# Attention's exponentials and values split into rounded parts and remainders, and a root moved ahead of a run of projection work

## What is computed

```python
def block(q):                                    # 128 queries
    s = einsum('bqkgd,bnkd->bkgqn', q, keys) * scale
    p = softmax(s)                               # over 1280 keys
    return einsum('bkgqn,bnkd->bqkgd', p, vals)
```

```python
o = rmsnorm(o_f + flip(o_b), gain)
return o * silu(g)
```

## Time and profile before

| | before |
|---|---|
| median of 3 runs | 3191.41 us |
| profiled execution | 3190.96 us, of which the span of the trace is 3189.1 us |
| granted TensorE clock, mean | 0.987 of full speed |
| DVE busy (VectorE) | 1543.6 us (48%) |
| ACT busy (ScalarE) | 1000.1 us (31%) |
| POOL busy (GpSimd) | 450.3 us (14%) |

### The profile page before, as it was taken

How to read it: one execution, slowest core, us unless ns; L and a number is a source line. 1 busy time by engine, 2 the same in 40 slices (tenths; PEclk the granted TensorE clock), 3 DMA queues, 4 the chain that set the end, 5 groups by cost and what they waited for, 6 DMA issues and landing times.

```text
span 3189.1 us, 36113 instructions
## 1 busy us (share of the span) xinstructions
PE 3046.8 (96%) x14927; PEld 2487.1 (78%) x14927; DVE 1543.6 (48%) x1907; ACT 1000.1 (31%) x1441; POOL 450.3 (14%) x352
## 2 busy tenths in 40 slices
PE   8899999989999999999989999999898999999997
PEld 6688888878788888888866668888776888888886
DVE  7566666553565553433566764456644122222224
ACT  5555555552311122212423332233322111111111
POOL 4333333321000001000300002133300000000001
PEclk9999999999999999999999999999999999999999
DMA  3111111122233431111210001101131111111111
GB/s 124 40 47 47 47 47 47 47 67 99 65 115 121 129 120 52 49 51 47 94 54 7 9 10 48 34 21 40 47 112 31 56 47 47 52 47 47 50 43 60
DMA packets 77235, 184.75 MB, mean 58 GB/s; under 512 B 7056, under 2 KB 29072, under 8 KB 77072
## 3 DMA queue, kind: packets, MB, share of 16 engines
q1 hardware_dynamic: 77072, 182.44, 18.2%
HBM read 163.87 MB, written 15.79 MB: 56 GB/s over the span
## 4 chain that ended last, share of the span: by engine, by line
PE 86%; DVE 8%; ACT 4%; issue 2%; POOL 0%; DMA 0%; POOLq 0%; DVEq 0%; SPq 0%; ACTq 0%
PE ps L512 39%; PE ps L1604 18%; PE ps L2950 8%; PE ps L2291 4%; DVE b L2899 2%; PE ps L2429 1%; PE ps L909 1%; PE ps L2255 1%; PE ps L2284 1%; PE ps L2283 1%; DVE b L501 1%; PE ps L916 1%; ACT b L493 1%; PE ps L86 1%; PE ps L891 1%
## 5 line engine op out<-in xcount | busy, mean ns | idle before, releaser
L512 PE MATMUL ps<-b 128*128 128x512 f32 x6024 | 1494.9, 399 | 35.6 <-DVE b L501 14.0
L512 PEld LDWEIGHTS ps<-b 128*128 128x128 f32 x6024 | 1109.9, 190 | 251.2 <-issue 19.9
L1604 PE MATMUL ps<-b 128*128 128x512 f32 x2592 | 599.1, 392 | 0.7 <-DVE b L1745 0.7
L1604 PEld LDWEIGHTS ps<-b 128*128 128x128 f32 x2592 | 485.0, 187 | 109.3 <-DVE b L1745 1.1
L501 DVE TENSOR_TENSOR b<-b 128x1024 fp32r<-128x1024 f32 (+1 forms) x206 | 255.3, 1241 | 288.3 <-ACT b L493 280.9
L493 ACT ACTIVATE b<-b 128x1024 fp32r<-128x1024 f32 (+1 forms) x206 | 214.9, 1045 | 515.9 <-PE ps L1604 427.4
L2950 PE MATMUL ps<-b 128*128 128x512 f32 (+1 forms) x1464 | 327.3, 379 | 6.8 <-ACT b L3010 5.9
L2950 PEld LDWEIGHTS ps<-b 128*128 128x128 f32 x1464 | 255.0, 192 | 56.5 <-issue 11.5
L1402 POOL TENSOR_TENSOR b<-b 128x1024 f32<-128x1024 f32 x18 | 43.2, 2399 | 916.8 <-ACT b L1433 916.4
L2291 PE MATMUL ps<-b 128*128 128x512 f32 x320 | 163.0, 592 | 0.0
L1761 DVE TENSOR_TENSOR b<-b,ps 128x1024 f32<-128x1024 f32 x64 | 78.1, 1220 | 152.4 <-PE ps L1604 152.3
(11 more groups left out here) (306 smaller groups left out, 3292.8 us busy)
## 6 DMA issues: line engine op xcount, KB each, us to landing
b<-in_down SPq DMA_DIRECT2D x52, 512.0 KB, 3.7
b<-in_mod SPq DMA_DIRECT2D x96, 256.0 KB, 2.7
b<-in_gu SPq DMA_DIRECT2D x44, 512.0 KB, 3.6
b<-scratch SPq DMA_DIRECT2D x38, 512.0 KB, 4.4
b<-in_dn_in SPq DMA_DIRECT2D x32, 512.0 KB, 5.1
b<-in_up SPq DMA_DIRECT2D x32, 512.0 KB, 3.8
b<-in_win SPq DMA_DIRECT2D x26, 512.0 KB, 3.7
scratch<-b SPq DMA_DIRECT2D x18, 512.0 KB, 2.9
```

The costliest lines, as they stand in the source:

```text
L512: ins = e.matmul(ps[:, c], w, h[:, k, c], start=first and k == 0 and i == 0, stop=last and k == KT - 1 and i == 2)
L1604: ins = e.matmul(ps[:, c], w, u[:, at[k], c], start=k == 0 and p == 0, stop=k == n - 1 and p == 2)
```

## The change

In the attention stage:

- The exponentials are taken twice: into an fp32 tile prob ("e") and into a rounded tile phi ("ex"). A subtraction makes the remainder plo = prob - phi ("lo"). VectorE does it for block 4 of every turn, behind the second half of the reciprocal; GpSimd does it for the other nine.
- The values are rounded when they are copied into vx, and VectorE makes their remainder vlo from PSUM in three subtractions at the start of `dve_attend`, behind a wait for all partition copies. GpSimd sets the middle of vlo to zero.
- The value matmul in fp32 becomes three in fp32r: vx with phi, vlo with phi, vx with plo; the third waits for "lo".
- Maxima 1 of the first turn wait for vlo instead of the copies.
- There are three phi and three plo tiles. The four prob tiles lie in two of the raw weight tiles, and SyncE loads the unit behind them after the stage. The reciprocal is written into the output tile ao, of which there is one, and the product is made in place.

In the gated attention, the six steps of projection work on ScalarE stand behind the root instead of ahead of its table.

```diff
+                self.phi, self.plo = ([sb([128, 512], F32R, at) for _ in range(3)] for _ in range(2))
+                self.vlo = sb([128, 10, 192], F32R, at)
+                self.ao = sb([128, 512], ctx=at)
+                free = [self.raw[(UNIT["win", 14] + i) % RAW] for i in range(2)]
+                self.prob = [r[:, 512 * i:512 * i + 512] for r in free for i in range(2)]
...
@@ pool_qkv
         self.after_qkv(e)
+        e.memset(self.vlo.bitcast(F32)[:, :, 64:128], 0.0).then_inc(*self.at[3].up("vz"))
@@ pe_attend
-                    e.wait_ge(*self.aq[1].at("tv", ("win", 5), 2))
+                    e.wait_ge(*V.at("vlo"))
...
-                e.matmul(O[i % 2], self.vx[:, b, 64 * g:64 * g + 128], self.prob[(t - 2) % 4], start=b == 0,
-                         stop=b == 9).then_inc(*P.up("pv", t - 2))
+                v, w = (x[:, b, 64 * g:64 * g + 128] for x in (self.vx, self.vlo))
+                e.matmul(O[i % 2], v, self.phi[(t - 2) % 3], start=b == 0, stop=False)
+                e.matmul(O[i % 2], w, self.phi[(t - 2) % 3], start=False, stop=False)
+                e.wait_ge(*(V if b in self.LOW else G).at("lo", t - 2))
+                e.matmul(O[i % 2], v, self.plo[(t - 2) % 3], start=False, stop=b == 9).then_inc(*P.up("pv", t - 2))
@@ act_attend
             if t >= 4:
-                e.wait_ge(*P.at("pv", t - 4))
-            e.activation(self.prob[t % 4], S[t % 3], ACT.Exp, scale=0.125).then_inc(*A.up("ex", t))
+                e.wait_ge(*(V if (t - 4) % 10 in self.LOW else G).at("lo", t - 4))
+            e.activation(self.prob[t % 4], S[t % 3], ACT.Exp, scale=0.125).then_inc(*A.up("e", t))
+            if t >= 3:
+                e.wait_ge(*P.at("pv", t - 3))
+            e.activation(self.phi[t % 3], S[t % 3], ACT.Exp, scale=0.125).then_inc(*A.up("ex", t))
+
+    LOW = (4,)
+
+    def attend_low(self, e, sig, t):
+        e.wait_ge(*self.at[1].at("ex", t))
+        if t >= 3:
+            e.wait_ge(*self.at[0].at("pv", t - 3))
+        e.tensor_tensor(self.plo[t % 3], self.prob[t % 4], self.phi[t % 3].bitcast(F32), ALU.subtract).then_inc(*sig.up("lo", t))
@@ dve_attend
+        for s in self.stack:
+            e.wait_ge(*s.end())
+        for j in range(3):
+            n = min(4, 10 - 4 * j)
+            e.wait_ge(*self.aq[1].at("tv", ("win", 5), j))
...
+            ins = e.tensor_tensor(parts(self.vlo), ps, parts(self.vx.bitcast(F32)), ALU.subtract)
+        ins.then_inc(*V.up("vlo"))
...
                 e.reciprocal(rec[r, 256:512], o[sums, 256:512]).then_inc(*V.up("rec", i - 1))
-                e.wait_ge(*V.last())
-                if i >= 5:
-                    e.wait_ge(*self.attst[(i - 1) % 4].at(i - 5, 1))
-                e.tensor_tensor(self.ao[((i - 1) // 2) % 2][r, :], o[r, :], rec[r, :], ALU.mult).then_inc(*V.up("of", i - 1))
+            if i < 16:
+                self.attend_low(e, V, 10 * i + 4)
+            if i:
+                e.wait_ge(*V.at("rec", i - 1))
+                e.tensor_tensor(self.ao[r, :], o[r, :], rec[r, :], ALU.mult).then_inc(*V.up("of", i - 1))
@@ pool_attend
             e.tensor_copy(self.qx[g][r], self.qs[g][r, :, qc].bitcast(F32)).then_inc(*G.up("qx", i))
+            e.wait_ge(*G.last())
+            for b in range(10):
+                if b not in self.LOW and i:
+                    self.attend_low(e, G, 10 * i - 10 + b)
+        for b in range(10):
+            if b not in self.LOW:
+                self.attend_low(e, G, 150 + b)
@@ act_gla
             e.activation(B["sq"], B["qf"], ACT.Square).then_inc(*A.up("osq", h))
-            side.fill(self.gla_fill(h, 6))
             self.act_roots(e, A)
             e.wait_ge(*V.at("oms", h))
             e.activation(small[:, 8:16], small[:, 0:8], ACT.Sqrt).then_inc(*A.up("ort", h))
+            side.fill(self.gla_fill(h, 6))
             side.until((h, "g"))
@@ SpSide
-        self.k.sp_weights(self.e, UNIT[u] + 5)
+        upto = UNIT[u] + 5
+        self.k.sp_weights(self.e, min(upto, UNIT["win", 14] + 3) if u[1] < 6 else upto)
```

More of the change, by code:

```diff
@@ L416, in memory @@
                 self.kx = [sb([128, TA], F32R, at, "right") for _ in range(2)]
-                self.vx = sb([128, 10, 192], ctx=at, side="right")
+                with ExitStack() as tmp:
+                    vz = sb([128, T], ctx=tmp, side="right")
+                self.vx = sb([128, 10, 192], F32R, at, "right")
                 self.amax, self.aneg = (sb([128, n], ctx=at, side="right") for n in (8, 72))
@@ L420, in memory @@
                     self.a_sq = [sb([128, T], ctx=tmp) for _ in range(2)]
-                    vz = self.vx.rearrange("p a b -> p (a b)")[:, 0:T]
                     z = [sb([128, TA], ctx=tmp), vz, sb([128, T], ctx=tmp)]
@@ L426, in memory @@
                 self.qx = [sb([128, 4, 128], F32R, at) for _ in range(2)]
-                self.prob = [sb([128, 512], ctx=at) for _ in range(4)]
-                self.ao = [sb([128, 512], ctx=at) for _ in range(2)]
-                self.arec = sb([128, 512], ctx=at)
+                self.phi, self.plo = ([sb([128, 512], F32R, at) for _ in range(3)] for _ in range(2))
[3 more added lines that the diff above has]
+                self.prob = [r[:, 512 * i:512 * i + 512] for r in free for i in range(2)]
             with ExitStack() as gl:
@@ L2198, in pool_qkv @@
         e.wait_ge(*A.at("tv", ("win", 5), 2))
-        e.memset(self.vx[:, :, 64:128], 1.0).then_inc(*G.up("fill"))
+        e.memset(self.vx.bitcast(F32)[:, :, 64:128], 1.0).then_inc(*G.up("fill"))
         self.after_qkv(e)
+        e.memset(self.vlo.bitcast(F32)[:, :, 64:128], 0.0).then_inc(*self.at[3].up("vz"))
     def attend_banks(self):
@@ L2220, in sp_attend @@
             e.wait_ge(*V.at("of", i))
-            ao = self.ao[(i // 2) % 2][r, :].rearrange("r (a p q) -> r a p q", a=2, p=2)
+            ao = self.ao[r, :].rearrange("r (a p q) -> r a p q", a=2, p=2)
             for p in range(2):
@@ L2280, in pe_attend @@
                     e.wait_ge(*self.aq[3].at("fill"))
+                    e.wait_ge(*G.at("vz"))
                 if t >= 3:
@@ L2296, in act_attend @@
         MX, MT, S, O = self.attend_banks()
+        j0 = UNIT["win", 14]
+        e.wait_ge(*self.ww.at(j0 + 1))
         for t in range(160):
@@ L2305, in dve_attend @@
         MX, MT, S, O = self.attend_banks()
-        mx, neg, rec = self.amax, self.aneg, self.arec
+        mx, neg, rec = self.amax, self.aneg, self.ao
         e.memset(neg, 0.0).then_inc(*V.up("neg"))
+        for s in self.stack:
[3 more added lines that the diff above has]
+            e.wait_ge(*self.aq[1].at("tv", ("win", 5), j))
+            ps = self.ps[:, 512 * j:512 * j + 128 * n].rearrange("p (b a m) -> p b a m", b=n, a=2)
+            parts = lambda ap: ap[:, 4 * j:4 * j + n, :].rearrange("p b (a m) -> p b a m", a=3)[:, :, 0:3:2, :]
+            ins = e.tensor_tensor(parts(self.vlo), ps, parts(self.vx.bitcast(F32)), ALU.subtract)
+        ins.then_inc(*V.up("vlo"))
         def maxima(i, j):
@@ L2339, in dve_attend @@
                 e.wait_ge(*P.at("pv", 10 * i - 1))
-                if i >= 2:
-                    e.wait_ge(*V.at("of", i - 2))
+                if i >= 3:
+                    e.wait_ge(*self.attst[(i - 3) % 4].at(i - 3, 1))
                 e.reciprocal(rec[r, 0:256], o[sums, 0:256])
@@ L2363, in pool_attend @@
             e.wait_ge(*(P.at("s", 10 * (i - 2) + 9) if i >= 2 else G.at("zero", g)))
+            if i >= 2:
+                e.wait_ge(*G.last())
             e.tensor_copy(self.qx[g][r], self.qs[g][r, :, qc].bitcast(F32)).then_inc(*G.up("qx", i))
+            e.wait_ge(*G.last())
+            for b in range(10):
[4 more added lines that the diff above has]
+                self.attend_low(e, G, 150 + b)
     GLA_ORDER = {"f": list(range(9)), "b": [1, 0, 9, 8, 7, 6, 5, 4, 3]}
```

## The result

| | before | after |
|---|---|---|
| median of 9 runs | 3192.84 us | 3183.99 us |
| range of 9 runs | 3189.16 to 3196.05 | 3176.68 to 3185.49 |
| profiled span | 3189.1 us | 3183.7 us |

The ratio is 0.997, with a 95% interval of 0.9962 to 0.9979: a gain of 0.3%, some 9 us, where 4.3 were forecast from a median of 3191.41. The gain is larger than the 6.4 us that the prediction took as the least to be told from no change, and to that it gave 0.20.

A forecast was written before the change was run, and what follows sets the result against it. TensorE (busy 96%) and VectorE's chain ahead of maxima 3 were taken to bound attention together. Terms -0.6 - 1.3 + 0.3 + 4.9 = +3.3 there and -7.6 in gated attention gave -4.3: 3187.1 us, range 3180 to 3205.

The forecast's parts named there:

- a middle turn under 15.3: Attention stage: sign that the prediction is wrong; it forecast 15.64 us for each middle turn, and over 15.9 also counted.
- a first negation not 4 to 6 late: Start of the attention stage: sign that the prediction is wrong; VectorE's first negation was forecast at 1670.8 instead of 1665.94.
- What bounds a turn: Middle turn of attention: VectorE's chain from first reciprocal to end of reduce 2 holds maxima 3; TensorE idles some 1.4 us.
- The size of a turn: Middle turn of attention: 15.64 us after the change, and 14 of them give 14 x -0.04 = -0.6 us.
- VectorE's 8.01: Middle turn: reciprocal A to the end of reduce 2, 7.29 us before, 8.01 with block 4's remainder added.
- my 7.61: Middle turn: from the end of reduce 2 to the next reciprocal A, 8.40 us before, less 0.85, plus 0.06.
- Start: Start of attention: VectorE makes vlo after all partition copies, then four reduces back to back; +4.9 us, covered by nothing.
- First turn: First turn of attention: no reciprocals, reduce 2 behind block 4's remainder, maxima 3 at 10.2 instead of 11.0; turn 14.4, -1.3 us.
- ScalarE and GpSimd: Middle turn: second exponentials fit at 12.0 us at most; GpSimd remainders take 1.20 each, 11.4 of 15.6, stalling TensorE 0.1.
- Root: Gated attention: table and root done before TensorE needs them, so three heads' waits of 2.5 us go; -7.6 us.
- The shared port: Rival, attention: GpSimd's remainder of block 7 delays VectorE's negation, each middle turn 1.2 us longer, 17 in all, 3204; chance 0.20.
- tail: Last turn of attention: 12.5 us and 0.5 for remainders meeting, against 13.2, then a chain 0.5 longer; together +0.3 us.

## Why the prediction was right

The time is in the range and the mechanism is the one that was told, but two of the prediction's own signs of being wrong were met: a middle turn under 15.3 (15.29), and a first negation not 4 to 6 late (9.6, of which 4.9 had come about before the stage). And errors of both signs stand in the sum.

- **What bounds a turn: right.** VectorE's chain ahead of maxima 3. Its remainder costs 0.66 to 0.72 a turn, and TensorE idles there, 1.42 at the loads in the turn shown, where 1.4 was forecast.
- **The size of a turn: missed by 0.35**, 15.64 against 15.29. Of VectorE's 8.01, the even turn had 8.00, but the odd one 7.71 (1818.66 to 1826.37), because three hand-overs are 0.1 tighter in it. I had read one even turn only; before, the odd ones have 7.17 beside 7.29. The other 0.2 is in my 7.61: measured 7.4. Maxima 3 now reach a TensorE that has run dry, so VectorE idles 0.94 ahead of reduce 3, not 1.10, and the row of shifts came in time (1799.86, with TensorE at the next maxima at 1800.13). Over 14 turns this is the term that was mis-sized: -5.6, not -0.6.
- **Start: right**, +4.7 against +4.9, counted from the first maxima. The copies that VectorE waits for are late with them.
- **First turn: wrong**, +0.9 against -1.3. Two steps failed. The -1.3 counts the forecast turn of 14.4 from a middle turn's 15.7, but the first turn of before takes 15.00: 0.7 of the miss. And I let the first exponential follow its scores at once. It stands behind the table load, and VectorE's remainder of block 4 stands ahead of reduce 2: it begins 11.06 after the first negation, and 10.22 with the table loaded ahead. That is 0.9 of the turn (15.90 to 14.98); 0.6 stays open. Before, nothing on VectorE waited for an exponential.
- **ScalarE and GpSimd: right.** A remainder takes 1.30, not 1.20, and still costs TensorE next to nothing: between 1692 and 1905 its matmuls wait only for the reduces (11.7 us, 14 times), its weight loads for GpSimd 30 times, 7.7 us in all.
- **Root: right in kind**, 7.6 of waits gone, nothing late behind them; the whole stretch gave 10.1. TensorE's other long waits there are those of before (5.9, 3.2 and 3.1 us), so the later load of the weights shows no cost in them.
- **The shared port** was priced at 1.2 a turn and cost 0.89 where it was provoked. It did not strike: the order of two starts was forecast with a margin of 0.1 and held with 0.03, so that it held in every turn is in part luck.
- The errors of -5.0 on the turns, -2.5 on the gated attention, +2.2 on the first turn and -0.7 on start and tail come to -6.0: the landmarks changed by -10.3, not -4.3. By the medians of 9 runs the gain was 8.9. That the time is only 3.1 below the forecast is in part because the first turn's error hides some of the others, and because the median of before, 3191.41 by 3 runs, is 3192.84 by 9.

## What to carry to other kernels

When a faster matmul form saves time, look first at which engine's chain between two hand-overs ends with it: here 27 us of saved matmul time came to 5.6 in the 14 middle turns, until 1.4 us of VectorE work a turn were moved out of its chain into its own idle gaps, which brought 16 us more there (a turn of 14.16 instead of 15.29). Work on an engine that has idle time left costs by its place in the queue, not by its amount. And read a repeated stage in two neighbouring turns before multiplying by their number.

## What was unexpected in the hardware

- A 128x4 instruction of VectorE that begins 0.17 us after the start of a GpSimd subtraction of 128x512 takes 1.16 us, and one that begins 0.03 ahead takes 0.17: the order of two starts decides over a microsecond.
- Two exponentials in a row from one bank begin 0.49 apart though each takes 0.60 (1680.65 and 1681.14 in the changed kernel).
- VectorE's hand-overs between instructions that stand side by side differ by 0.1 us from one turn to the next (1808.29 to 1809.01, but 1823.64 to 1824.29). The turns differ in the half of the partitions that the sums and products use. Why that matters was not tried.
